# The 31-tap convolution moved from VectorE and GpSimd onto TensorE as diagonal 32x32 tiles, and the linear attention one unit earlier

## The reference, cut to what matters

```python
p_all = u @ w_in
ya = conformer_conv(...)   # A: GLU, 31-tap depthwise convolution, layer norm, silu
yb = gla_mixer(...)        # B: gated linear attention in chunks of 64
yc = short_conv(...)       # C: 3-tap gated convolution
yd = fox_prompt / fox_decode(...)   # D: attention with a forget gate
h = h + rms_norm(concat([ya, yb, yc, yd]) @ w_out, m_post)

# conformer_conv
a = val * jax.nn.sigmoid(gate)
xpad = jnp.concatenate([buf, a], axis=1)             # 30 old rows ahead
y = causal_depthwise(xpad, conv_w) + conv_b          # y[t, c] = sum_k xpad[t + k, c] * w[k, c]
y = jax.nn.silu(layer_norm(y, ln_g, ln_b))
```

## Time and profile before

| | us |
|---|---|
| runs of the kernel before | 1146.12, 1155.79, 1156.91 (median 1155.79) |
| the profiled execution | 1149.1 |
| its span, first to last instruction | 1147.3 |
| mean granted TensorE clock over the span | 0.985 |

### The profile page before, as it was taken

One profiled execution on the slowest core, in us unless ns is written; L12 is line 12 of the kernel. 1 busy time (PEld: TensorE's weight loads), 2 busy tenths in 40 slices (PEclk: granted clock), 3 DMA queues, 4 the chain that ended last, 5 costly groups with the idle time before them and its releaser, 6 DMA issues.

```text
span 1147.3 us, 25988 instructions
## 1 busy us (share of the span) xinstructions
PE 1078.0 (94%) x8956; PEld 1034.5 (90%) x8956; DVE 753.4 (66%) x986; ACT 564.2 (49%) x906; POOL 356.6 (31%) x449
## 2 busy tenths in 40 slices
PE   6999999888989999999989999998888899999995
PEld 6999999786779999999889999997767889999995
DVE  5666644789986766654566665439899576666446
ACT  6544454552256644454454445436423566444544
POOL 3222211326933322221122222014476352222212
PEclk9999999998899999999999999999989999999998
DMA  7655576251525455555535555853334256555552
GB/s 264 213 180 178 185 218 202 96 169 47 183 85 187 143 188 183 183 172 182 163 120 181 181 181 185 253 174 115 109 106 135 75 169 202 184 181 176 177 182 75
DMA packets 64778, 188.73 MB, mean 165 GB/s; under 512 B 9626, under 2 KB 20898, under 8 KB 64546
## 3 DMA queue, kind: packets, MB, share of 16 engines
q1 hardware_dynamic: 64674, 187.38, 51.0%
HBM read 183.97 MB, written 3.38 MB: 163 GB/s over the span
## 4 chain that ended last, share of the span: by engine, by line
PE 74%; DVE 13%; issue 9%; ACT 3%; DMA 0%; DVEq 0%; SPq 0%; POOL 0%; ACTq 0%; POOLq 0%
PE ub L291 15%; PE ub L293 15%; PE ub L292 15%; PE quad L291 8%; PE quad L292 8%; PE quad L293 8%; DVE resid L959 2%; DVE w_lo L278 2%; DVE z_t L956 2%; DVE yg L1038 1%; DVE proj L1209 1%; ACT w_hi L272 1%; PE ub L311 1%; PE ub L313 1%; PE ub L312 1%
## 5 line engine op out<-in xcount | busy, mean ns | idle before, releaser
L278 DVE TENSOR_TENSOR w_lo<-raw,w_hi 128x1024 fp32r<-128x1024 f32 x339 | 450.1, 1332 | 350.5 <-ACT w_hi L272 350.1
L272 ACT ACTIVATE w_hi<-raw 128x1024 fp32r<-128x1024 f32 x339 | 346.5, 1028 | 288.2 <-PE ub L293 196.7
L291 PE MATMUL ub<-hg_hi,w_hi 128*128 128x264 f32 x960 | 280.7, 292 | 2.4 <-DVE proj L1209 2.4
L292 PE MATMUL ub<-hg_lo,w_hi 128*128 128x264 f32 x960 | 276.1, 288 | 0.0
L293 PE MATMUL ub<-hg_hi,w_lo 128*128 128x264 f32 x960 | 275.8, 287 | 0.0
L291 PE MATMUL ub<-act_hi,w_hi 128*128 128x264 f32 x704 | 200.5, 285 | 0.0
L293 PE MATMUL ub<-act_hi,w_lo 128*128 128x264 f32 x704 | 200.0, 284 | 0.0
L291 PE MATMUL quad<-hg_hi,w_hi 128*128 128x264 f32 x688 | 196.9, 286 | 3.0 <-DVE w_lo L278 3.0
L292 PE MATMUL ub<-act_lo,w_hi 128*128 128x264 f32 x704 | 199.1, 283 | 0.0
L292 PE MATMUL quad<-hg_lo,w_hi 128*128 128x264 f32 x688 | 195.6, 284 | 0.0
L293 PE MATMUL quad<-hg_hi,w_lo 128*128 128x264 f32 x688 | 195.5, 284 | 0.0
(11 more groups left out here) (258 smaller groups left out, 1420.0 us busy)
## 6 DMA issues: line engine op xcount, KB each, us to landing
raw<-in_w_gu SPq DMA_DIRECT2D x179, 512.0 KB, 4.0
raw<-in_w_dn SPq DMA_DIRECT2D x64, 512.0 KB, 4.0
raw<-in_w_in SPq DMA_DIRECT2D x44, 512.0 KB, 3.7
raw<-in_w_dn SPq DMA_DIRECT2D x32, 384.0 KB, 3.6
raw<-in_w_out SPq DMA_DIRECT2D x16, 512.0 KB, 3.3
pages<-in_cache_k SPq DMA_DIRECT2D x32, 128.0 KB, 3.4
pages<-in_cache_v SPq DMA_DIRECT2D x32, 128.0 KB, 3.0
con<-in_con SPq DMA_DIRECT2D x1, 1448.0 KB
```

What stands on the lines that cost most here:

```text
L272: eng.activation(w_hi[:, slot, 0:w], raw[:, slot, 0:w], ACT.Copy).then_inc(*sig("hi_ready", reps))
L278: eng.tensor_tensor(w_lo[:, slot, 0:w], raw[:, slot, 0:w], w_hi[:, slot, 0:w].bitcast(F32), ALU.subtract)\
L291: eng.matmul(out, a_hi, x_hi[:, k0 + k, :], start=(first and k == 0), stop=False)
L292: eng.matmul(out, a_hi, x_lo[:, k0 + k, :], start=False, stop=False)
```

## The change: what it does

- The 62 shifted multiply-adds per layer on DVE and POOL, and the join, are gone. In their place stand 248 fp32 matmuls per layer on PE: for each channel tile c, row group q (32 channels) and tap t, a 32x32 diagonal weight tile times the 32x256 slice of `a_pad` that begins at t. Tap t goes to column group t mod 4, so that each of the 16 (row, column) groups of the array sums every fourth tap of its 32 channels, and each row group has a PSUM bank of its own. They stand at step 12, behind the transposes of the linear attention.
- The diagonal tiles `cw` (128 x 1984) are made by POOL at step 0 from a small constant (`eye`) and the weights, between the clearing of `a_pad` and that of `qm`. They lie in `proj` tiles that are not in use until later.
- ACT copies the four PSUM banks to `c_part` at step 13; `conv_join` on PE sums the four column groups (4 matmuls of 512 columns) at step 13; ACT adds the bias at step 14.
- All of the linear attention moves up by one step on PE, ACT and DVE: levels at steps 5 to 11, transposes at 12, updates at 13, outputs at 15. Decode scores move to steps 13 and 14; `qm` and `qd` stay at 14.
- Units 6 to 9 are in another order (both gates ahead of the values), and the two sigmoids with their table loads are at step 8 in place of 10.
- Sum, variance, normalization and silu of the convolution come at steps 15 to 21 in place of 21 to 24. The output projection begins with groups B and A, then C and D. The 12 transposes of the prompt attention go to four banks in place of two, without a wait between them.

```diff
-ALR, FG, BQ, BK, AV, AG, BG, BV, DQ, DKK, DVV, CB, CC, CX = 0, 1, 2, 3, 4, 6, 8, 10, 12, 14, 16, 18, 19, 20
+ALR, FG, BQ, BK, AG, BG, AV, BV, DQ, DKK, DVV, CB, CC, CX = 0, 1, 2, 3, 4, 6, 8, 10, 12, 14, 16, 18, 19, 20
-YB, YC, YD, YA = 0, 2, 4, 6
+YB, YA, YC, YD = 0, 2, 4, 6
+        cw = proj[:, DVV:24, :].rearrange("p a b -> p (a b)")[:, 0:2 * TAPS_A * 32].rearrange("p (c t m) -> p c t m", c=2, t=TAPS_A)
+        c_part = sb("c_part", [P, 4, 2 * TP])
...
+            def conv_taps(l):
+
+                for c in range(2):
+                    for step in range(8):
+                        for q in range(4):
+                            for j in range(4):
+                                t, r = 4 * step + j, slice(32 * q, 32 * q + 32)
+                                if t < TAPS_A:
+                                    mm = pe.matmul(quad[32 * j:32 * j + 32, 512 * q + TP * c:512 * q + TP * (c + 1)], cw[r, c, t, :], a_pad[r, c, t:t + TP],
+                                                   start=step == 0, stop=t + 4 >= TAPS_A)
+                mm.then_inc(*sig("a_conv"))
+
+            def conv_join(l):
+
+                after(l, a_ev=4, b_vt=1)
+                for q in range(4):
+                    mm = pe.matmul(mb[2][32 * q:32 * q + 32, :], const("eye", 32), c_part[:, q, :], start=True, stop=True)
+                mm.then_inc(*sig("a_join"))
...
-                if 6 <= n <= 12:
-                    gla_level(l, n - 6)
+                if 5 <= n <= 11:
+                    gla_level(l, n - 5)
+                if n == 12:
+                    gla_tokens(l)
+                    conv_taps(l)
                 if n == 13:
-                    gla_tokens(l)
-                if n == 14:
+                    conv_join(l)
                     gla_updates(l)
                     decode_scores(l, 0)
...
-                if n == 14:
-
+                if n == 13:
+
+                    after(l, a_conv=1)
+                    for q in range(4):
+                        act.activation(c_part[:, q, :], quad[:, 512 * q:512 * (q + 1)], ACT.Copy).then_inc(*sig("a_ev"))
...
-            def conv_taps(l, first, last):
-                for t in range(first, last):
-                    for c in range(2):
-                        k = 2 * t + c
-                        y, x, w = ymix[:, YA + c, 0:TP], a_pad[:, c, t:t + TP], par[:, PAR["acw"] + c * TAPS_A + t:PAR["acw"] + c * TAPS_A + t + 1]
...
-                            dve.scalar_tensor_tensor(y, x, w, y, ALU.mult, ALU.add).then_inc(*sig("a_tap"))
...
+                    pool.tensor_tensor(cw[:, :, :, :].rearrange("p c t m -> p (c t) m"), const("eye", 32).unsqueeze(1).to_broadcast([P, 2 * TAPS_A, 32]),
+                                       par[:, PAR["acw"]:PAR["acw"] + 2 * TAPS_A].unsqueeze(2).to_broadcast([P, 2 * TAPS_A, 32]), ALU.mult).then_inc(*sig("a_cw"))
                     zero = con[:, 0:H * NT].rearrange("p (a b) -> p a b", a=H)
                     pool.tensor_tensor(qm[:, :, :], zero, zero, ALU.subtract).then_inc(*sig("d_qz"))
```

More of the change, by code:

```diff
@@ L842, in mix @@
                                .then_inc(*sig("d_qd"))
-                if n == 17:
+                if n == 14:
+                    after(l, a_join=1)
+                    for c in range(2):
+                        act.activation(ymix[:, YA + c, 0:TP], mb[2][:, c * TP:(c + 1) * TP], ACT.Identity,
+                                       bias=par[:, PAR["acb"] + c:PAR["acb"] + c + 1]).then_inc(*sig("a_all"))
+                if n == 16:
                     after(l, b_o=1)
@@ L851, in mix @@
                     act.activation(ymix[:, YB:YB + 2, TP:NT], mb[2][:, 0:16].rearrange("p (b j) -> p j b", j=2), ACT.Copy).then_inc(*sig("b_og"))
+                if n == 17:
+                    after(l, a_cen=2)
+                    act.activation(a_sqr, ymix[:, YA:YA + 2, :], ACT.Square).then_inc(*sig("a_sq"))
                 if n == 18:
+                    after(l, b_gn=1)
+                    for j in range(2):
+                        act.activation(o_rs[:, j, :], mb[j][:, 0:NT], ACT.Ln, bias=biases[:, 0:1], scale=1.0 / DV).then_inc(*sig("b_rs"))
+                    after(l, a_var=1)
+                    act.activation(a_rs[:, :], ub[3][:, 0:NT], ACT.Ln, bias=biases[:, 0:1], scale=1.0 / 256).then_inc(*sig("a_rsd"))
+                    for j in range(2):
+                        after(l, b_rs=j + 1)
+                        act.activation(o_rs[:, j, :], o_rs[:, j, :], ACT.Exp, scale=-0.5).then_inc(*sig("b_rs"))
+                    after(l, a_rsd=1)
+                    act.activation(a_rs[:, :], a_rs[:, :], ACT.Exp, scale=-0.5).then_inc(*sig("a_rsd"))
+                if n == 17:
                     after(l, b_og=3)
@@ L864, in mix @@
                     act.activation(ptd[:, :, :].rearrange("p g r -> p (g r)"), mb[3][:, 0:TP], ACT.Copy).then_inc(*sig("d_ptd"))
[L865 to L869, removed]
-                        act.activation(o_rs[:, j, :], o_rs[:, j, :], ACT.Exp, scale=-0.5).then_inc(*sig("b_rs"))
                     after(l, d_mx=2)
@@ L895, in mix @@
                                        bias=par[:, PAR["alb"] + c:PAR["alb"] + c + 1]).then_inc(*sig("a_y"))
+                if n == 22:
+                    round_mixed(l, YB)
+                    for h in range(H):
+                        probabilities(l, h)
+                if n == 23:
+                    round_mixed(l, YA)
+                    after(l, d_o=1)
+                    act.activation(ymix[:, YD:YD + 2, 0:TP], mb[2][:, :].rearrange("p (a b) -> p a b", a=2), ACT.Copy).then_inc(*sig("d_y"))
             def round_mixed(l, first):
@@ L904, in probabilities @@
                 after(l, d_pT=h + 1)
-                act.activation(smT[:, h, :], mb[h % 2][:, 0:3 * P], ACT.Copy).then_inc(*sig("d_pt"))
+                act.activation(smT[:, h, :], fox_bank[h][:, 0:3 * P], ACT.Copy).then_inc(*sig("d_pt"))
             def mixer(l):
@@ L919, in outp @@
                     output_tile(l, 1, n, ub[n % 4], n % 2, reps)
-                for first in range(2, KD, 2):
+                for first in (YC, YD):
                     round_mixed(l, first)
```

177 lines of the change are left out of this document (69 added, 108 removed).

## The result

| | us, median | runs |
|---|---|---|
| before | 1155.4 | 4 (1146.1 to 1156.9) |
| changed | 1165.6 | 4 (1165.4 to 1165.8) |

By these medians the changed kernel is 10.2 us slower. The ratio on record is 1.0127, 95% interval 1.0083 to 1.0171; it puts before at 1151.0, near the median of all 91 of its runs, 1150.7, and the loss at 14.6 us. I had forecast 1152, next to no change. The time lies in the range, but a loss of over 1% had a chance of only 0.27. The profiled execution has a span of 1163.7 us, 16.4 more than that of before.

The account below looks back on a forecast made before the run. PE alone bounds the feed-forward, DVE the level stage. Per layer -3.2 - 0.8 + 3.9 = -0.1 us, -0.2 for both, gives 1149; forecast 1152, between the profiled execution and the 1155.8 median; range 1134 to 1168.

Parts of the forecast that it names:

- The convolution, 6.9 us: Tile matmuls on PE's path, per layer: 16 tiles at once, 32 x 0.216 = 6.9 us.
- that case: Rival at 1158: convolution takes 10.1 us, 3.2 more per layer, as tiles start less tightly; chance 0.08.
- The rival at 1165: Convolution on PE runs only eight tiles at once, 13.4 us; decides from about 12.7; chance 0.17 including four at once.
- The level stage, 3.9 us: Stage ahead of unit 12's end, DVE taken as the bound: 3.9 us more per layer.
- The lock: Level stage: POOL building `cw` takes turns with DVE, a whole instruction each, and costs 3.1 us.
- The move by one unit: Level stage: one level more ahead of unit 12, priced at 0.8 us.
- Behind unit 12, -3.2: From unit 12's end to the output projection: 76.6 us becomes 73.4, 3.2 us less per layer.
- The wait at decode scores: Behind unit 12: PE waits 1.5 us for `qd` in place of 3.5.
- Transposes and `pm`: Behind unit 12: transposes no longer share banks, their 2.5 us wait goes; `pm` causes no wait.
- Output projection, -0.8: Output projection: group A follows B at once and covers PE's idle time, 0.8 us less per layer.
- The clock in the convolution: Forecast: stays at full clock. Rival at 1162: falls inside the convolution, 5.1 us per layer; chance 0.10.
- The base: Time of the kernel before: profiled execution 1149.1 us, median of the runs shown 1155.8.

Follow-up runs that it names:

- the five versions with early weights: Changed kernel with the diagonal weights built in the first feed-forward's down projection, 1156.9 us alone; the other versions add further edits.

## Why the prediction was wrong, point by point

- **The convolution, 6.9 us: the step that failed.** It took 12.76 us in layer 0 and 12.2 in layer 1, 5.9 and 5.3 more, 11.2 of the 16.4 us between the profiled runs. I took full overlap of 16 tiles from rows that show it for 4, and the issue of 8.7 ns per pass from a row with 32 passes. Two things took its place. The first is the pace: without the stops 10.8 us are left, 3.9 too many, 21.8 ns per pass, a factor of 107 / 10.8 = 9.9 (the Trainium skill's 10.6, in TensorE: Matmul & The Clock Gate, Part 3, is close, and I gave that case 0.08). The starts in the trace show why the row with 32 passes misled: at the head of the convolution and behind each stop the first 32 passes go at about 7 ns within a round of sixteen, 0.24 us a round; from then on most are 16 to 17 ns apart, with 0.16 us more every 34 passes. What sets that pace, no run shows. The second are the stops, 1.96 us: 992 instructions at one go arrive too slowly, which no row with few instructions can show. This is the harder bound, since with half of the columns the passes went faster and the convolution did not. The rival at 1165 came out in its time, and near its point of decision (12.7), by luck: its eight tiles at once were not the limit.
- **The level stage, 3.9 us.** It took 6.3 and 6.5. The lock was right as a mechanism and, at 3.1, nearly in size: by the medians it costs 3.0 to 4.4 per layer in the changed kernel and 3.4 in the kernel before; how much of that is the low clock behind it stays open. The move by one unit I priced at 0.8, since I held DVE to be the bound "back to back". But DVE idles there for `w_hi`, 4.4 us in layer 0 before and 7.1 in the changed kernel, and `w_hi` waits for a free slot, which waits for PE (12.3 and 16.1 us). With one unit less before the first level, PE gets a wait of 2.4 us, and low clock behind it in most layers. In the five versions with early weights the stage is 2.4 to 4.4 us longer than before: 2.4 to 2.6 where no low clock falls into it, 3.2 to 3.5 with 3.4 us of it, 3.9 and 4.4 with twice that. Which link of that ring is decisive stays open: reordering DVE only moved the wait.
- **Behind unit 12, -3.2.** It became +3.3 in layer 0 and +1.9 in layer 1. Of the difference of 6.5 in layer 0, 5.9 are the convolution, 0.1 the join (1.0 for 0.9), 1.7 the longer low clock, and PE idles less than I allowed, 1.5 us beside the stops in place of 2.5; the terms add up to 6.7. The wait at decode scores was 1.4 for 1.5. Transposes and `pm` went as said, and DVE is under 50% busy.
- **Output projection, -0.8.** 1.0 less, no idle time left: right.
- **The clock in the convolution** stayed high, as I argued. With half the columns it fell inside it, at about 278 in layer 0; how near the whole columns were to that, no run shows.
- **The base.** I forecast 1152 as next to nothing against the 1155.8 of three runs. All 91 runs on record have a median of 1150.7, so three runs of a kernel that scatters by 1% put the base 5 us too high.

## What to carry to other kernels

Before many small tile matmuls go onto TensorE, count instructions, not only passes: here 256 arrived per 3.4 to 4.0 us, and a run of up to 320 of them ahead of a full-size unit had no stop. A pace read from 32 passes is that of a burst. Work moved off an engine is worth what its waits cost, not its busy time; sharing the taps so that neither engine waits gave the gain that moving all of them did not. An instruction of 3.5 us on POOL beside a busy DVE cost about its own length, 3.0 to 4.4 us of the kernel's time by the medians.

## What the runs showed of the hardware

- Instruction delivery as a bound for TensorE: 11.5 to 12.8 us for 992 instructions in a row on sixteen tiles, with whole or half columns. Each of 21 stops ends 1.30 to 1.55 us behind the end of an instruction packet.
- Tile matmuls in fp32 of 256 columns: 26.6 ns per pass with eight tiles in turn and no stop, 21.8 with sixteen, stops left out; the first 32 passes of a burst about 7 ns apart within a round of sixteen, later ones 16 to 17.
- With half-width tile matmuls the granted clock fell inside the convolution (0.50 from 278.4 on); with whole width it stayed at 1.00 throughout.
- A `w_lo` of 1.20 us on DVE took 4.27 to 4.53 us beside a POOL instruction of 3.5 us.
- The kernel before scatters by 1% from run to run (1146 to 1159 us); the changed kernel by 0.03% in four runs.
